# Splitting a weight block before, and not after, the results of the running block are worked on, in a two-layer decoder trunk

## Chip, cores and metric

The kernel runs on one core of a Trainium2 chip (trn2). The metric is the device time of one execution in microseconds. Before the change it is 1976.48 us, the median of three runs (1976.42 to 1977.69).

## What is computed

Two layers of a decoder trunk on 256 tokens of width 1024, all in fp32. Each layer adds a token mixer, a cross attention and a feed-forward part to the residual x:

```python
for layer in range(2):
    h = rms_norm(x, norm_mix[layer])
    x = x + token_mixer(h, ...)              # h @ w_in, four branches A to D, gates, w_branch, w_out
    h = rms_norm(x, norm_cross[layer])
    m = rms_norm(mem, norm_mem[layer])
    x = x + memory_cross_attention(h, m, w_xq[layer], w_xkv[layer], w_xo[layer])
    h = rms_norm(x, norm_ffn[layer])
    x = x + (swiglu(...) if layer == 0 else moe_ffn(...))     # dense, d_ff 3584; then top 2 of 8 experts
return rms_norm(x, norm_final)
```

The branches of the mixer are A sliding-window attention, B attention over 64 selected keys per query, C retention and D pooling. Nearly all the work is the products of 256 token rows with weight matrices, some 530 MB of fp32 that are read once.

## The kernel before

**Blocks.** The weights come in blocks of 512 rows by 512 columns, 128 partitions by 2048 fp32 or 1 MB. `plan_chunks` and `plan_dense` write out their order: 60 mixing blocks of layer 0, 42 dense blocks, 60 mixing blocks of layer 1, and then the experts' jobs. All of the first 162 stand in `PLANNED`; block n uses slot n mod 6 of the buffers `raw` and `w_hi`.

**Precision.** A product is made of three fast matmuls. ScalarE copies a block to the rounded type, w_hi (`hi`, L871, signalled by `hi_done`). VectorE writes the rest, raw less w_hi, back in place (`lo`, L1391, `lo_done`). The moving or stationary operand, kept in `stat0` and `stat1`, is split the same way. TensorE then adds x_hi w_hi, x_hi w_lo and x_lo w_hi (`product`, L2254 to L2256): 24 matmuls for a block (32 for the eight "turned" chunks xk0 to xk3 and xq0 to xq3 of each layer, L2629 and L2631).

**What sets the order.** Each engine runs its own program in its order. TensorE counts finished blocks in `block_used`. SP's queue issues the load of block n+5 as soon as block n-1 is used up (`load_block`, L628 and L629), since that frees the slot. `hi` of block n+5 waits for its landing and for the same count. SP does nothing else in between, apart from a few loads of small inputs.

**A step.** For each block n ScalarE and VectorE have a step. It consists of the work on results that belongs to it and of the split of block n+5 (`LEAD` is 5). The work is written out by hand in `work` (L1068) and `dense_work` (L1208) for ScalarE and in `work_of` (L1758) and `dense_work` (L1924) for VectorE. It holds, for instance:

- evacuating the accumulators of a chunk once its last block is used up (`evac`, `gates_out`, `gated`, `residual`, and `rotate` for the rotary chunks);
- the steps of softmax between TensorE's small matmuls (`soft_start`, `exps`, `soft_end` with the scaling L1631, `soft_out` with the copy L1640);
- splitting operands that TensorE has just transposed (`split_gain` L1463, `split_pair` L1495, `split_mem` L1503, `split_pool` L1472, `hidden_split` L1921), which later blocks or the next one use.

TensorE does its small matmuls and transposes at fixed places: in the middle of a block (`within`, `dense_within`) or behind it (`after`). Before each it waits for the bank (`opened`, `emptied`) or the operand (`ready`). Small results share four banks in turn, so a bank can be used again only when its reader of four uses before is through. Examples that matter below:

- xo1's second block turns x's first half in its middle (f0, f1); the dense block g0 behind it waits for them to be split. f2 and f3 are turned behind g0's first block and waited for by its second.
- d5's second block turns the last hidden units in its middle, and d6 uses them. d6's second block turns h0 and h1, and layer 1's first block, pu, waits for these.
- xk0 uses the memory rows, split in the steps of upA1 and upB1; its second half waits for the latter.
- behind upD0 TensorE makes the scores of a1; its second pair of banks needs the copy of a0's output.
- xkv3's second block is followed by xo0, which uses xt0 and xt1; xo1's first block is followed by xo0's second, which uses xt2 and xt3.

ScalarE's loop over a layer's blocks ends like this (L1338 to L1350), and VectorE's (L2199 to L2212) is built in the same way:

```python
for c, i in ORDER:
    if c.name in TURNED:
        hi_planned(layer * LAYER_BLOCKS + c.numbers[i] + LEAD)
    work(layer, c.name, i)
    ...
    if c.name not in TURNED and (layer, c.name, i) != (DEPTH - 1, "xo1", 1):
        hi_planned(layer * LAYER_BLOCKS + c.numbers[i] + LEAD)
```

So only the turned chunks split block n+5 first. From block 162 on `hi_planned` splits the first experts' blocks; VectorE's splits of those stand in `first_expert_lows` with a lead of four, and `lo_planned` does nothing there.

Of the kernel before, what the change touches and what calls it, by code (L numbers as in the profile page):

```python
# [50 lines left out]
TURNED = [f"x{w}{n}" for w in "kq" for n in range(4)]  # L51
SLOTS = 6
CYCLE = 6
LEAD = 5
# [97 lines left out]
def build(nc, x_in, mem_in, positions, norm_mix, w_in, attn_sink, w_branch, w_out, pool_w, pool_scale,  # L152
          norm_cross, norm_mem, w_xq, w_xkv, w_xo, norm_ffn, dense_w_gu, dense_w_down, router_w,
          moe_w_gu, moe_w_down, norm_final, out):
    DEPTH, D = norm_mix.shape
# [13 lines left out]
    MIX_BLOCKS = len(ORDER)  # L169
    FFN_BLOCKS = UNITS * UNIT_BLOCKS  # L170
    LAYER_BLOCKS = MIX_BLOCKS + FFN_BLOCKS
# [7 lines left out]
    with ctx:  # L179
# [314 lines left out]
        def dense_block(which, u, i):  # L494
            return (0, MIX_BLOCKS + DENSE.index((which, u, i)))
# [81 lines left out]
        def used_at(b):  # L577
            return number(b) + (1 + SLOTS)
# [287 lines left out]
        def _(act):  # L866
            def hi(b, width=UNIT):

                act.wait_ge(raw_landed[slot(b)], landed_at(b))
                act.wait_ge(block_used, number(b) + 1)  # L870
                act.activation(w_hi[:, slot(b), :, 0:width], raw[:, slot(b), :, 0:width], ACT.Copy).then_inc(hi_done, 1)  # L871

            def expert_hi_of(b):

                act.wait_ge(raw_landed[slot(b)], landed_at(b))
                act.wait_ge(block_used, number(b) + 1)
                act.activation(expert_hi(b), expert_raw(b), ACT.Copy).then_inc(hi_done, 1)  # L877

            def hi_planned(n):

                if n >= len(PLANNED):
                    expert_hi_of((EXPERTS_BASE, n - len(PLANNED)))
                    return
                layer, c, i = PLANNED[n]
                if layer == "dense":
                    hi((0, n))
                    return
                if c.name == "kv":
                    act.wait_ge(kv_landed[i], (layer + 1) * 16)
                if c.name[:3] in ("upA", "upB"):  # L890
                    act.wait_ge(up_landed[int(c.name[3])], (2 * layer + "AB".index(c.name[2]) + 1) * 16)
                hi((0, n), c.n)
# [9 lines left out]
            def norm_scale(layer, name, junk):  # L902
                square_sum(x, junk, norm_act, layer, f"{name} sq")
                root_of_mean(norm_act, norm_dve, layer, f"{name} sq")

            def split_gain(layer, name, dst, kind, q):

                act.wait_ge(small_full.sem, full_at(layer, name))
                for i, k in enumerate((2 * q, 2 * q + 1)):
                    ins = act.activation(dst[:, 0, k, :], small(layer, name)[:, i * T:(i + 1) * T], ACT.Copy,  # L910
                                         scale=gain_at(layer, kind, k))
                ins.then_inc(act_hi.sem, 1)
# [295 lines left out]
            def dense_work(which, u, i):  # L1208

                if (which, u, i) == ("u", 0, 0):  # L1210
                    split_gain(0, "f2", stat0, "ffn", 2)
                    split_gain(0, "f3", stat0, "ffn", 3)
                    norm_scale(0, "ffn", tok)
                if which == "g" and i == 1:
                    if u == 0:
                        act.wait_ge(norm_dve.sem, norm_dve.at(0, "ffn inv"))
                    else:
                        act.wait_ge(dense_hid.sem, dense_hid.at(u - 1, "hid"))
                    act.wait_ge(block_used, used_at(dense_block("g", u, 1)))
                    for t in range(NT):  # L1220
                        ins = act.activation(silu_g[:, t, :], bank[t][:, :], ACT.Silu, scale=rs_ffn[:, t:t + 1])
                    ins.then_inc(dense_silu.sem, 1)
                    if u:
                        hidden_turned(u - 1, 4)
                if (which, u, i) == ("d", UNITS - 2, 1):
                    hidden_turned(UNITS - 1, 0)
                if (which, u, i) == ("d", UNITS - 1, 1):
                    split_gain(1, "h0", stat0, "mix", 0)
                    split_gain(1, "h1", stat0, "mix", 1)

            def hidden_turned(u, first):

                act.wait_ge(dense_tr.sem, dense_tr.at(u, "tr"))
                for t in range(NT):
                    src = bank[first + t][:, :].rearrange("p (k n) -> p k n", k=4)
                    ins = act.activation(hidden_t(0, u)[:, :, t * P:(t + 1) * P], src, ACT.Copy)
                ins.then_inc(dense_hi.sem, 1)
# [99 lines left out]
            hi_planned(4)  # L1337
            for layer in range(DEPTH):  # L1338
                for c, i in ORDER:
                    if c.name in TURNED:  # L1340
                        hi_planned(layer * LAYER_BLOCKS + c.numbers[i] + LEAD)
                    work(layer, c.name, i)
                    if layer == 0:
                        first_layer_extras(c.name, i)
                    if c.name not in TURNED and (layer, c.name, i) != (DEPTH - 1, "xo1", 1):
                        hi_planned(layer * LAYER_BLOCKS + c.numbers[i] + LEAD)
                if layer == 0:
                    for n, step in enumerate(DENSE):
                        dense_work(*step)
                        hi_planned(MIX_BLOCKS + n + LEAD)  # L1350

            act.wait_ge(norm_dve.sem, norm_dve.at(1, "ffn inv"))
            act.activation(tok[:, 0, :], x[:, 0, :], ACT.Copy, scale=rs_ffn[:, 0:1])
# [33 lines left out]
        def _(dve):  # L1387
# [6 lines left out]
            def lo_planned(n):  # L1394

                if n >= len(PLANNED):
                    return
                layer, c, i = PLANNED[n]
                lo((0, n), UNIT if layer == "dense" else c.n)
# [524 lines left out]
            def dense_work(which, u, i):  # L1924

                if (which, u, i) == ("u", 0, 0):
                    split_gain(0, "f2", stat0, "ffn", 2)
                    split_gain(0, "f3", stat0, "ffn", 3)
                    dve.wait_ge(acc_free[CH["xo1"].parity].sem, acc_free[CH["xo1"].parity].at(0, "xo1"))
                    scale_of_rows(x, tok, rs_ffn, norm_dve, norm_act, 0, "ffn ")  # L1930
                if which == "g" and i == 1 and u:
                    hidden_split(u - 1, 4)
                if which == "u" and i == 1:
                    dve.wait_ge(dense_silu.sem, dense_silu.at(u, "silu"))
                    dve.wait_ge(block_used, used_at(dense_block("u", u, 1)))
                    if u:
                        dve.wait_ge(dense_tr.sem, dense_tr.at(u - 1, "tr"))
                    for t in range(NT):
                        ins = dve.scalar_tensor_tensor(out=hid[:, t, :], in0=bank[2 + t][:, :], scalar=rs_ffn[:, t:t + 1],
                                                       in1=silu_g[:, t, :], op0=ALU.mult, op1=ALU.mult)  # L1940
                    ins.then_inc(dense_hid.sem, 1)
                if which == "d":
                    if (u, i) == (UNITS - 2, 1):
                        hidden_split(UNITS - 1, 0)
                    if (u, i) == (UNITS - 1, 1):
                        split_gain(1, "h0", stat0, "mix", 0)
                        split_gain(1, "h1", stat0, "mix", 1)
                    dve.wait_ge(block_used, used_at(dense_block("d", u, i)))
                    for t in range(NT):
                        xs = x[:, t, i * 512:(i + 1) * 512]  # L1950
                        ins = dve.tensor_tensor(xs, xs, bank[4 + 2 * i + t][:, :], ALU.add)
                    ins.then_inc(dense_acc.sem, 1)
# [246 lines left out]
            for layer in range(DEPTH):  # L2199
                for c, i in ORDER:  # L2200
                    if c.name in TURNED:
                        turned_sum(layer, c.name)
                        lo_planned(layer * LAYER_BLOCKS + c.numbers[i] + LEAD)
                    work_of(layer, c.name, i)
                    if c.name not in TURNED:
                        lo_planned(layer * LAYER_BLOCKS + c.numbers[i] + LEAD)
                    if (layer, c.name, i) != (DEPTH - 1, "xo1", 1):
                        first_expert_lows(layer * LAYER_BLOCKS + c.numbers[i])
                if layer == 0:
                    for n, step_ in enumerate(DENSE):  # L2210
                        dense_work(*step_)
                        lo_planned(MIX_BLOCKS + n + LEAD)  # L2212

            route()
            first_expert_lows(len(PLANNED) - 1)
# [671 lines left out]
```

## Time and profile before

| | us |
|---|---|
| median of the runs | 1976.48 |
| the profiled execution | 1977.02 |
| its span, first to last instruction | 1974.8 |
| TensorE's matmuls busy | 1959.9 (99%) |
| VectorE busy | 1534.9 (78%) |
| ScalarE busy | 1251.4 (63%) |
| mixing and dense blocks of the trace | 8 to 1005 |
| experts | 1013 to 1964 |

The span is one execution as the hardware profiler saw it. The time of that execution is 2.2 us longer, for what lies around the instructions. Busy time is an average: what a change is worth is read at the place where it acts, from the waits and the order of events there. In the rows below, L871 is a line of the kernel, PE is TensorE, ACT ScalarE, DVE VectorE, and SPq SP's queue; a bracket at the end of a row gives the engine's idle time before it and what ended that.

### The profile page before, as it was taken

The numbers are of one execution on the slowest core, as the hardware profiler recorded it, in microseconds if no ns is written. First come the engines' busy times: TensorE is split into PE (matmuls) and PEld (weight loads), VectorE is DVE, ScalarE is ACT, GpSimd is POOL, SyncE is SP. The second block draws the span as 40 slices with busy tenths as digits, with TensorE's granted clock in tenths as the row PEclk, the third lists the DMA queues.
The fourth block names the chain that finished last, engine by engine and source line by source line (L and its number), as shares of the span: only waits on it lengthen the run. The fifth ranks groups of instructions, "written<-read, shape, count | busy, mean of one in ns | idle before, by whom it ended". The sixth has DMA issues, their size and how long they took to land.

```text
span 1974.8 us, 25344 instructions
## 1 busy us (share of the span) xinstructions
PE 1959.9 (99%) x9380; PEld 1626.1 (82%) x9380; DVE 1534.9 (78%) x1445; ACT 1251.4 (63%) x1235; POOL 105.7 (5%) x164
## 2 busy tenths in 40 slices
PE   8999999999999999999999999999999999999998
PEld 7887888888888887788878888888888888888886
DVE  7877667655555777777669988989888988988996
ACT  6566545454434456655566777877767776776775
POOL 4300000000000210000000100100000000000030
PEclk9999999999999999999999999999999999999999
DMA  8544655455555544566479999999999999999995
GB/s 290 163 150 149 179 191 171 149 182 188 185 191 182 171 150 156 164 204 215 154 267 362 378 400 382 388 372 379 387 374 397 364 389 386 364 392 380 385 393 201
DMA packets 203698, 539.16 MB, mean 273 GB/s; under 512 B 10265, under 2 KB 34401, under 8 KB 203617
## 3 DMA queue, kind: packets, MB, share of 16 engines
q1 hardware_dynamic: 200784, 529.38, 74.3%
q0 software_dynamic: 2304, 8.39, 1.2%
q8 instruction: 53, 0.87, 0.2%
q10 hardware_dynamic: 528, 0.29, 0.0%
q14 instruction: 29, 0.23, 0.0%
HBM read 529.64 MB, written 8.39 MB: 272 GB/s over the span
## 4 chain that ended last, share of the span: by engine, by line
PE 98%; DVE 1%; ACT 0%; DMA 0%; issue 0%; SPq 0%; DVEq 0%; ACTq 0%
PE bank L2701 15%; PE bank L2699 15%; PE bank L2700 15%; PE bank L2254 13%; PE bank L2256 13%; PE bank L2255 13%; PE bank L2631 3%; PE bank L2302 2%; PE bank L2629 1%; PE bank L2778 1%; PE bank L2320 1%; PE bank L2342 1%; PE bank L2713 0%; PE bank L2711 0%; PE bank L2712 0%; PE bank L2793 0%
## 5 line engine op out<-in xcount | busy, mean ns | idle before, releaser
L877 ACT ACTIVATE w_hi<-raw 128x2048 fp32r<-128x2048 f32 x336 | 628.6, 1922 | 122.5 <-DMA raw<-in_moe_w_gu 80.6
L1410 DVE TENSOR_TENSOR expert_lo<-raw,w_hi 128x2048 fp32r<-128x2048 f32 x280 | 630.2, 2294 | 20.6 <-ACT w_hi L877 20.5
L2699 PE MATMUL bank<-w_hi,stat 128*128 128x512 f32 x1312 | 514.2, 392 | 0.0
L2701 PE MATMUL bank<-w_hi,stat 128*128 128x512 f32 x1312 | 511.0, 390 | 0.0
L1391 DVE TENSOR_TENSOR low_in_place<-raw,w_hi 128x2048 fp32r<-128x2048 f32 (+1 forms) x161 | 367.5, 2285 | 134.9 <-ACT w_hi L871 134.4
L2254 PE MATMUL bank<-w_hi,stat 128*128 128x512 f32 (+1 forms) x1168 | 458.3, 392 | 0.0
L2255 PE MATMUL bank<-low_in_place,stat 128*128 128x512 f32 (+1 forms) x1168 | 453.1, 388 | 0.0
L2256 PE MATMUL bank<-w_hi,stat 128*128 128x512 f32 (+1 forms) x1168 | 453.1, 388 | 0.0
L871 ACT ACTIVATE w_hi<-raw 128x2048 fp32r<-128x2048 f32 (+1 forms) x161 | 305.8, 1904 | 220.5 <-DMA raw<-in_dense_w_gu 60.2
L2700 PE MATMUL bank<-expert_lo,stat 128*128 128x512 f32 x1088 | 423.4, 389 | 0.0
L2701 PEld LDWEIGHTS bank<-w_hi,stat 128*128 128x128 f32 x1312 | 246.2, 188 | 51.6
L2699 PEld LDWEIGHTS bank<-w_hi,stat 128*128 128x128 f32 x1312 | 246.3, 188 | 49.8
L2254 PEld LDWEIGHTS bank<-w_hi,stat 128*128 128x128 f32 x1168 | 219.7, 188 | 49.9 <-issue 6.0
L2256 PEld LDWEIGHTS bank<-w_hi,stat 128*128 128x128 f32 x1168 | 219.7, 188 | 45.2
L2255 PEld LDWEIGHTS bank<-low_in_place,stat 128*128 128x128 f32 x1168 | 219.9, 188 | 42.7
L2700 PEld LDWEIGHTS bank<-expert_lo,stat 128*128 128x128 f32 x1088 | 204.3, 188 | 41.7
L1410 DVE TENSOR_TENSOR area_low<-raw,w_hi 128x2048 fp32r<-128x2048 f32 x56 | 130.2, 2326 | 0.2
L1991 DVE TENSOR_TENSOR stat<-bank,stat 128x512 fp32r<-128x512 f32 x56 | 36.5, 687 | 74.4 <-ACT stat L1277 74.3
L2700 PE MATMUL bank<-area_low,stat 128*128 128x512 f32 x224 | 87.2, 389 | 0.0
L1248 ACT ACTIVATE area<-bank 128x512 f32<-128x512 f32 x56 | 30.9, 596 | 87.8 <-PE bank L2701 87.8
L2631 PE MATMUL bank<-stat,w_hi 128*128 128x512 f32 x256 | 68.7, 395 | 0.0
L844 POOL COPY token_now<-slot_token 128x1 int32 x7 | 13.0, 1860 | 816.0 <-PE bank L2793 589.7
(346 smaller groups left out, 1438.7 us busy)
## 6 DMA issues: line engine op xcount, KB each, us to landing
raw<-in_moe_w_gu SPq DMA_DIRECT2D x224, 1024.0 KB, 7.5
raw<-in_moe_w_down SPq DMA_DIRECT2D x112, 1024.0 KB, 8.4
raw<-in_w_in SPq DMA_DIRECT2D x55, 1024.0 KB, 4.9
raw<-in_dense_w_gu SPq DMA_DIRECT2D x28, 1024.0 KB, 5.1
raw<-in_w_xkv SPq DMA_DIRECT2D x16, 1024.0 KB, 5.3
raw<-in_dense_w_down SPq DMA_DIRECT2D x14, 1024.0 KB, 5.1
raw<-in_w_branch SPq DMA_DIRECT2D x8, 1024.0 KB, 5.0
raw<-in_w_branch SPq DMA_DIRECT2D x16, 512.0 KB, 7.0
```

What stands on the lines that cost most here:

```text
L871: act.activation(w_hi[:, slot(b), :, 0:width], raw[:, slot(b), :, 0:width], ACT.Copy).then_inc(hi_done, 1)
L877: act.activation(expert_hi(b), expert_raw(b), ACT.Copy).then_inc(hi_done, 1)
L1391: dve.tensor_tensor(in_place_lo(b)[:, :, 0:width], raw[:, slot(b), :, 0:width], f32_of(w_hi[:, slot(b), :, 0:width]), ALU.subtract).then_i ...
L1410: dve.tensor_tensor(expert_low(b), expert_raw(b), f32_of(expert_hi(b)), ALU.subtract).then_inc(lo_done, 1)
L2254: pe.matmul(dst, x_hi, wh, start=start, stop=False)
L2255: pe.matmul(dst, x_hi, wl, start=False, stop=False)
L2256: return pe.matmul(dst, x_lo, wh, start=False, stop=stop)
L2302: ins = pe.transpose(b[:, i * P:(i + 1) * P], src, ident[:, :])
L2631: ins = pe.matmul(whole, wh[:, k, cols], moving[:, 0:2, k, :], start=(k == 0), stop=(k == KD - 1))
L2699: pe.matmul(dst[:, :], x_hi, wh[:, at], start=start, stop=False)
L2700: pe.matmul(dst[:, :], x_hi, wl[:, at], start=False, stop=False)
L2701: ins = pe.matmul(dst[:, :], x_lo, wh[:, at], start=False, stop=stop)
```

## The change

In both loops the split of block n+5 now stands ahead of step n's work for all mixing and dense blocks. For the turned chunks nothing changes. Instructions, buffers and semaphores stay what they were, and so do TensorE's, SP's and GpSimd's programs.

```diff
--- before.py
+++ after.py
@@ -1337,17 +1337,15 @@
             hi_planned(4)
             for layer in range(DEPTH):
                 for c, i in ORDER:
-                    if c.name in TURNED:
+                    if (layer, c.name, i) != (DEPTH - 1, "xo1", 1):
                         hi_planned(layer * LAYER_BLOCKS + c.numbers[i] + LEAD)
                     work(layer, c.name, i)
                     if layer == 0:
                         first_layer_extras(c.name, i)
-                    if c.name not in TURNED and (layer, c.name, i) != (DEPTH - 1, "xo1", 1):
-                        hi_planned(layer * LAYER_BLOCKS + c.numbers[i] + LEAD)
                 if layer == 0:
                     for n, step in enumerate(DENSE):
+                        hi_planned(MIX_BLOCKS + n + LEAD)
                         dense_work(*step)
-                        hi_planned(MIX_BLOCKS + n + LEAD)
 
             act.wait_ge(norm_dve.sem, norm_dve.at(1, "ffn inv"))
             act.activation(tok[:, 0, :], x[:, 0, :], ACT.Copy, scale=rs_ffn[:, 0:1])
@@ -2200,16 +2198,14 @@
                 for c, i in ORDER:
                     if c.name in TURNED:
                         turned_sum(layer, c.name)
-                        lo_planned(layer * LAYER_BLOCKS + c.numbers[i] + LEAD)
+                    lo_planned(layer * LAYER_BLOCKS + c.numbers[i] + LEAD)
                     work_of(layer, c.name, i)
-                    if c.name not in TURNED:
-                        lo_planned(layer * LAYER_BLOCKS + c.numbers[i] + LEAD)
                     if (layer, c.name, i) != (DEPTH - 1, "xo1", 1):
                         first_expert_lows(layer * LAYER_BLOCKS + c.numbers[i])
                 if layer == 0:
                     for n, step_ in enumerate(DENSE):
+                        lo_planned(MIX_BLOCKS + n + LEAD)
                         dense_work(*step_)
-                        lo_planned(MIX_BLOCKS + n + LEAD)
 
             route()
             first_expert_lows(len(PLANNED) - 1)
```

## Rows read from the trace of the kernel before

**Rows 1.** The page: busy time by engine; the chain that ended last, by engine

```profile
PE 1959.9 (99%) x9380; PEld 1626.1 (82%) x9380; DVE 1534.9 (78%) x1445; ACT 1251.4 (63%) x1235; POOL 105.7 (5%) x164
...
PE 98%; DVE 1%; ACT 0%; DMA 0%; issue 0%; SPq 0%; DVEq 0%; ACTq 0%
```

**Rows 2.** Waits of TensorE: for what, us in total, times, longest

```profile
PE bank L2302 <- DMA x<-in_x: 3.2, 2, 1.7
...
PE bank L2629 <- DVE stat L1503: 0.5, 2, 0.3
```

**Rows 3.** Timeline, two dense blocks, SP's queue, ScalarE, VectorE (start us, us, what)

```profile
441.18 0.37 SPq L629 DMA_DIRECT2D raw<-in_dense_w_down  x1
...
446.62 0.37 SPq L629 DMA_DIRECT2D raw<-in_dense_w_down  x1
...
446.22 1.92 ACT L871 ACTIVATE w_hi<-raw 128x2048 fp32r<-128x2048 f32 x1 [3.49 <-DMA raw<-in_dense_w_down]
...
448.17 2.29 DVE L1391 TENSOR_TENSOR low_in_place<-raw,w_hi 128x2048 fp32r<-128x2048 f32 x1 [0.26 <-ACT w_hi L871]
```

**Rows 4.** The page's DMA issues: count, size, median us to landing

```profile
raw<-in_dense_w_gu SPq DMA_DIRECT2D x28, 1024.0 KB, 5.1
```

**Rows 5.** Timeline, first dense blocks of layer 0, SP's queue and VectorE

```profile
395.85 0.37 SPq L629 DMA_DIRECT2D raw<-in_dense_w_gu  x1
...
402.18 0.37 SPq L629 DMA_DIRECT2D raw<-in_dense_w_gu  x1
...
399.76 1.66 DVE L1463 SCALAR_TENSOR_TENSOR stat<-bank,gains,stat 128x256 fp32r<-128x256 f32 x4
```

**Rows 6.** Timeline, last dense blocks, SP's queue, ScalarE, VectorE

```profile
608.92 0.37 SPq L629 DMA_DIRECT2D raw<-in_w_in  x1
...
614.97 1.92 ACT L871 ACTIVATE w_hi<-raw 128x2048 fp32r<-128x2048 f32 x1 [1.36 <-DMA raw<-in_w_in]
...
613.64 1.29 DVE L1921 TENSOR_TENSOR stat<-bank,stat 128x512 fp32r<-128x512 f32 x2 [2.02 <-ACT stat L1236]
```

**Rows 7.** Timeline, the end of layer 0's mixing blocks, SP's queue and VectorE

```profile
256.50 0.37 SPq L629 DMA_DIRECT2D raw<-in_w_out  x1
...
262.02 1.29 DVE L1672 TENSOR_TENSOR gate<-bank,gate 128x512 f32<-128x512 f32 x2
263.23 1.66 DVE L1503 SCALAR_TENSOR_TENSOR stat<-memT,gains,stat 128x256 fp32r<-128x256 f32 x4
```

**Rows 8.** Attention in layer 1: VectorE's timeline, then the chain (start us, us)

```profile
746.05 0.68 DVE L1640 COPY o_buf<-bank 128x512 f32<-128x512 f32 x1
...
761.94 2.29 DVE L1631 TENSOR_TENSOR area<-area,sinv 128x2048 f32<-128x2048 f32 x1
...
745.87 2.15 PE bank L2320 x16
...
764.58 2.62 PE bank L2302 x24
...
818.01 1.79 PE bank L2302 x16
```

**Rows 9.** Timeline, cross attention in layer 0, SP's queue and VectorE

```profile
355.58 0.37 SPq L629 DMA_DIRECT2D raw<-in_dense_w_gu  x1
...
364.82 0.37 SPq L629 DMA_DIRECT2D raw<-in_dense_w_gu  x1
...
374.07 1.28 DVE L1495 TENSOR_TENSOR stat<-bank,stat 128x512 fp32r<-128x512 f32 x2
```

**Rows 10.** TensorE's first products, its last matmuls, and the end's stretch with granted clock

```profile
8.18 0.77 PE L2254 MATMUL bank<-w_hi,stat 128*128 128x512 f32 x1
...
12.17 0.39 PE L2254 MATMUL bank<-w_hi,stat 128*128 128x512 f32 x1
...
1965.41 1.88 PE L2815 MATMUL bank<-heads_t,expert_lo 128*128 128x512 f32 x4
...
1960.00:1972.00 12.00, 7.23 (x28) 4.66 (x26) 6.19 (x11) 5.72 (x12) 0.00 (x0) 0.97 0.08 31
```

## Prediction, made before the changed kernel was run

> **What bounds the kernel now.** The page comes first. TensorE is busy for 99% of the span and carries 98% of the chain that ended last [rows 1], so a block of weights costs what its matmuls cost, and the change can gain only where TensorE waits. The waits of TensorE are next. They come to 7.3 us in six entries, and nearly all of it is the wait for the first inputs at the kernel's start (the 3.2 us of [rows 2] and an entry of 2.5 us like it); the largest that a result block sets is the 0.5 us on the split memory rows, L1503 [rows 2]. So the question is not what the change frees, but which of the hidden steps stay hidden.
>
> Then the order of events in one dense block, on which all else rests [rows 3]. The load of block n+5 is issued when block n-1 is used up, at 441.18; the next one, 5.44 us later, marks the end of block n (24 matmuls). The load takes 5.0 us to land: ScalarE's split starts at 446.22, released by the DMA, and takes 1.92 us. VectorE's split starts at 448.17 and takes 2.29 us. The median over the 28 dense loads is 5.1 us [rows 4]. So the split of block n+5 is **not work that lies ready while block n is multiplied**: its data land some 0.4 us before block n ends. That decides the case.
>
> **The change, step by step.** Counted from that issue, ScalarE is through the split at +7.0 us and VectorE at +9.3 us (5.0 + 1.92 + 2.29 and the hand-overs), or 1.5 and 3.8 us after the end of block n. Before, ScalarE and VectorE did step n's results as soon as they were there, and then the split. Afterwards neither touches step n's results before those times. Removed and added instructions: none. Moved: one activation (1.92 us) and one subtraction (2.29 us) per step, for all but the eight turned chunks of each layer, which had this order already. No DMA moves, since a load waits only for its block to be used; SP's and POOL's queues are passed by nothing. The split itself is early by four blocks in either order: free. Behind the new waits stand the evacuations, softmax steps and operand splits of step n, and TensorE waits for these in program order. I walked through its waits; most have a block or more of room. In the steady dense blocks, for instance, the hidden splits end 5.2 us after g's second block and are asked for two blocks (11 us) later: nothing. These have no such room:
>
> 1. **Operands made in the last block before they are used, 19.1 us.** Rows f0, f1 are turned in the middle of xo1's second block, split, and used by the next block. A block with eight transposes takes 6.3 us [rows 5], VectorE's split of the rows 1.66 us [rows 5]. From the issue, the operand is ready at 9.3 + 1.66 = 10.9 us and wanted at 6.3: 4.6 us. The same holds for f2, f3 one dense block on (4.6), and for h0, h1 ahead of layer 1 (4.6). The last hidden units, used by d6, wait for a load that landed only 6.05 us after its issue [rows 6]: 6.05 + 1.92 + 2.29 + 1.29 = 11.6 against 6.3, so 5.3 us.
> 2. **Split of the memory rows for xk0, 7.6 us.** The load is issued at 256.50 [rows 7]; VectorE's split of it would end at 265.8; then come the gating (1.29) and the split (1.66), together until 268.7. They ended at 264.9. TensorE waited for exactly this before (L1503, [rows 2]), so all of 3.8 us shows, in both layers.
> 3. **Attention chains, 8.6 us.** After upD0, TensorE's second pair of score banks (1.1 us into the 2.15 us that begin at 745.87) needs the copy L1640, which began at 746.05 and would now end at 749.0: 2.1 us. The normalised scores of a1 were ready at 764.2 for transposes at 764.58 [rows 8]; with the split ahead of them they come 1.0 us late, beyond the 2.1. For b1 the transposes at 818.01 had 0.2 us of room, and by the same sum come 1.2 us late. Times two layers.
> 4. **Cross attention, 5.2 us.** The split of xt0, xt1 is asked for 9.2 us after the issue of block 60 (355.58 to 364.82, [rows 9]) and is ready at 9.4 + 1.29: 1.6 us. That of xt2, xt3 comes at 10.6 against 8.2 us: 2.4 us. The residual after them adds 0.2. In layer 1 VectorE's expert splits are not moved, only ScalarE's: 1.0 in place of 4.2.
> 5. **Single ones, 2.1 us.** Layer 0's memory transposes need a bank that split_pool frees (1.5 us); layer 1's out0 residual had 0.1 us left (0.6).
>
> The sum is 42.6 us. Where a stall stands, the loads issued before it have landed by its end, so it is not paid twice; I took each from its own issue.
>
> **TensorE's clock** is the one resource that the change may touch and that the middle of the trace doesn't show. At the start the nine products from 8.18 to 12.17 were paced at 0.43 us, the 1.2 GHz level, against 0.226 later: 2.0 us lost. At the end the last matmuls were over at 1967.3, and the mean granted clock of 0.97 in 1960 to 1972 puts the fall to half at about 1971.3, 4.0 us later [rows 10]. Four of the stalls above (4.6, 4.6, 4.6, 5.3) are longer than that, two (3.8) nearly so. Bounds: no fall, nothing, or six falls at twice the price of the start, 24 us. Lying close to the 4.0 us, I take two falls of four, 3.9 us. By the Trainium skill ("TensorE: Matmul & The Clock Gate", "HAM oscillation — how this bites in real kernels"), an engine that waits idle for its data is sent back to the slow clock at every such wait, and pays the warm-up each time. By that rule all four long ones fall, and the sum is 4 us more than mine; no row here shows a stall in mid-kernel that would tell.
>
> The profiled execution took 1977.02 us (span 1974.8, 2.2 around it): 1977.0 + 42.6 + 3.9 = 2023.5. The median is 0.5 lower, so I say 2023.
>
> **The rivals.** *(a) Room everywhere, no change, about 1976.5.* Loads would have to land well before a block's end, or the waits have slack that I overlooked. For it: TensorE now waits hardly anywhere, and of some hundred steps I find a dozen short. Against it: the room at places 2 and 3 is 0 to 0.2 us by the rows, and 3.8 us of delay can't vanish in that. 4%. *(b) Faster or at least not slower.* The split would fill time in which ScalarE and VectorE wait for the block's end, and leave them free right behind it, where the 1.92 and 2.29 us used to stand ahead of the next step. Price: at most the 1.6 us of TensorE's waits that lie behind its start, so 1975. It decides if the load lands more than 4.2 us before the block's end; it lands 0.4 us before it [rows 3]. 2%. *(c) The clock falls at every long stall and takes long to return.* 42.6 + 24 gives 2043. For it the 4.0 us of [rows 10]; against it that matmuls follow without a break, and that a slow stretch gives VectorE time to catch up. It is what the rule of the Trainium skill named above would come to at its worst. 14%. *(d) Only the straight chains of places 1 and 2 stall* (26.7 us), since attention and cross attention take back in the next step what they lose: 2004. 12%. The forecast has 68%.
>
> **How the numbers follow.** The forecast's own range is 2010 to 2034: a fifth of the 42.6 up and down (each stall is a small difference of two long sums), and 0 to 4 falls of the clock. To leave out no more than 2 in 10 the range takes in the nearer half of (c) and of (d): 2007 to 2040. 0.2% (4 us) is about what a measurement can tell. Slower by more than that: the forecast, (c) and (d), 0.94; within it, (a) and most of (b), 0.05; faster, 0.01.
>
> **What would show it.** In the waits of TensorE: new entries for L1503 (7 to 8 us in all), L1463 (14), L1921 (5), L1495 (4 to 6), L1640 (4) and L1631 (4). ScalarE's split then waits on the DMA, and step n's evacuations begin 1.4 us after the block's end. Steady dense blocks keep their 5.44 us. A clock below full speed in the stretches behind f1, f3, d6 and layer 1's pu tells of the falls. I am wrong if TensorE's waits stay under 10 us, or if dense blocks grow all along, which would mean that the results' delay compounds from step to step.

## The result, and the profile after

The changed kernel takes **2047.13 us**, the median of five runs (2045.67 to 2049.09), against 1976.69 for the kernel before in the same comparison: 1.0354 times as long, with a 95% interval of 1.0343 to 1.0366. That is 70.4 us slower, where 46.5 had been forecast; the range ended at 2040. The profiled execution took 2045.9 us, with a span of 2043.7.

The page first: busy time, the chain that ended last, and the two groups of the split (busy, mean ns; after the bar the engine's idle time before them and what ended it).

```profile
PE 1981.5 (97%) x9380; PEld 1639.6 (80%) x9380; DVE 1535.1 (75%) x1445; ACT 1252.6 (61%) x1235; POOL 105.5 (5%) x164
...
PE 89%; DMA 4%; DVE 3%; ACT 2%; SPq 1%; issue 1%; POOL 0%; DVEq 0%; ACTq 0%
...
L1389 DVE TENSOR_TENSOR low_in_place<-raw,w_hi 128x2048 fp32r<-128x2048 f32 (+1 forms) x161 | 370.6, 2302 | 292.6 <-ACT w_hi L871 292.0
L871 ACT ACTIVATE w_hi<-raw 128x2048 fp32r<-128x2048 f32 (+1 forms) x161 | 306.0, 1900 | 461.0 <-DMA raw<-in_w_in 134.0
```

The same two groups on the page of the kernel before:

```profile
L1391 DVE TENSOR_TENSOR low_in_place<-raw,w_hi 128x2048 fp32r<-128x2048 f32 (+1 forms) x161 | 367.5, 2285 | 134.9 <-ACT w_hi L871 134.4
L871 ACT ACTIVATE w_hi<-raw 128x2048 fp32r<-128x2048 f32 (+1 forms) x161 | 305.8, 1904 | 220.5 <-DMA raw<-in_dense_w_gu 60.2
```

The work is the same: VectorE and ScalarE are busy to within 1.2 us of [rows 1], with as many instructions. Their idle time ahead of the splits has more than doubled. And the chain that was TensorE's for 98% is its own for only 89%; DMA, VectorE and ScalarE have entered it. Two numbers split the loss. TensorE's idle time (span less busy) grew from 14.9 to 62.2 us, **47.3 us of waits**. Its busy time grew by **21.6 us** with the same 9380 matmuls, for which a slower clock and the refilling of a stopped engine are the candidates. Together they are the 68.9 us between the spans.

The waits of TensorE (for what; us in total, times, longest). Lines of VectorE's and TensorE's programs stand two to four lower than before the change.

```profile
PE bank L2250 <- DVE stat L1461: 13.7, 3, 4.7
PE bank L2298 <- DVE area L1629: 9.8, 4, 3.9
PE bank L2625 <- DVE stat L1501: 7.7, 2, 3.9
PE bank L2250 <- DVE stat L1919: 5.3, 1, 5.3
PE bank L2316 <- DVE o_buf L1638: 4.7, 2, 2.3
PE bank L2250 <- DVE stat L1493: 4.4, 3, 2.5
...
PE bank L2298 <- POOL gate L799: 2.3, 1, 2.3
```

In [rows 2] the only line of this kind was the memory rows', with 0.5 us. Every line named in the prediction is here, and five of the six come out within an us of their forecast (14, 7 to 8, 5, 4, 4 to 6). The sixth, L1629, was to be 4 and is 9.8.

One dense wait in full, from the timelines of SP's queue, ScalarE, VectorE and TensorE (start us, us, what; a bracket is the idle time before and what ended it). It is the wait for f0, f1, place 1 of the prediction.

```profile
412.95 1.03 PE L2298 MATMUL bank<-ident,x 128*128 128x128 f32 x8
...
415.56 1.91 ACT L871 ACTIVATE w_hi<-raw 128x2048 fp32r<-128x2048 f32 x1 [7.85 <-DMA raw<-in_dense_w_gu]
417.38 1.55 ACT L910 ACTIVATE stat<-bank,gains 128x256 fp32r<-128x256 f32 x4
...
417.50 2.29 DVE L1389 TENSOR_TENSOR low_in_place<-raw,w_hi 128x2048 fp32r<-128x2048 f32 x1 [5.79 <-ACT w_hi L871]
419.71 1.65 DVE L1461 SCALAR_TENSOR_TENSOR stat<-bank,gains,stat 128x256 fp32r<-128x256 f32 x4
...
421.42 0.80 PE L2250 MATMUL bank<-w_hi,stat 128*128 128x512 f32 x1 [4.70 <-DVE stat L1461]
```

ScalarE stood idle for 7.85 us until the load had landed; VectorE waited 5.79 us for ScalarE; only then was the operand split that the next block needed. The rows had been turned by 414.0 (the first line), and the block before ended at 416.7. So ScalarE stood idle for 1.6 us more, and VectorE, which needs ScalarE's part first, for 3.5, while the urgent work lay behind a wait.

**The clock.** The stretches in which the granted clock (PEclk) stood at half, by windows; the columns are the window, its length, busy us of PE, PEld, DVE, ACT and POOL, PEclk, DMA share, GB/s.

```profile
138.00:141.40 3.40, 3.40 (x11) 2.32 (x8) 3.23 (x6) 2.40 (x2) 0.00 (x0) 0.51 0.05 19
213.20:219.90 6.70, 4.88 (x20) 4.59 (x21) 3.97 (x2) 5.04 (x8) 0.00 (x0) 0.50 0.34 129
281.50:288.20 6.70, 5.66 (x18) 4.78 (x19) 2.26 (x5) 1.40 (x1) 0.00 (x0) 0.50 0.00 0
404.40:407.70 3.30, 3.30 (x10) 2.53 (x9) 0.00 (x0) 1.90 (x1) 0.00 (x0) 0.50 0.18 69
421.40:424.70 3.30, 3.28 (x8) 2.61 (x9) 2.06 (x3) 1.91 (x1) 0.00 (x0) 0.50 0.02 5
438.50:445.20 6.70, 5.46 (x13) 4.30 (x14) 3.30 (x8) 3.38 (x3) 0.00 (x0) 0.50 0.16 61
660.40:667.10 6.70, 6.11 (x14) 4.81 (x15) 3.15 (x4) 0.51 (x1) 0.00 (x0) 0.50 0.00 0
680.90:684.20 3.30, 3.30 (x9) 2.57 (x8) 1.94 (x2) 1.86 (x1) 0.00 (x0) 0.50 0.00 0
947.10:950.40 3.30, 3.30 (x11) 2.61 (x11) 0.00 (x0) 0.00 (x0) 2.98 (x5) 0.50 0.24 98
```

Nine falls, each of 3.4 or 6.8 us, 44 us in all. TensorE was busy for 38.7 us of these windows (the PE column added up), so by an estimate half of that, 19 us of the 21.6, went to the clock. This is one execution; the mean granted clock was 0.988 in it and 0.986 to 0.989 in the other four. From 1010 to 2036, through layer 1's last mixing blocks and all experts, TensorE was at full clock and busy for 1024.3 of the 1026 us.

### The profile page after: what moved, and what is told of

The parts are those of the page before. It is cut to its first block, busy times and chain, and to the rows that moved or that the text cites. A ratio compares the mean times of both kernels' runs of the same rounds, so it can differ in the third digit from the quotient of the medians.

```text
span 2043.7 us, 25344 instructions
## 1 busy us (share of the span) xinstructions
PE 1981.5 (97%) x9380; PEld 1639.6 (80%) x9380; DVE 1535.1 (75%) x1445; ACT 1252.6 (61%) x1235; POOL 105.5 (5%) x164
## 4 chain that ended last, share of the span: by engine, by line
PE 89%; DMA 4%; DVE 3%; ACT 2%; SPq 1%; issue 1%; POOL 0%; DVEq 0%; ACTq 0%
PE bank L2697 15%; PE bank L2695 15%; PE bank L2696 15%; PE bank L2250 11%; PE bank L2252 11%; PE bank L2251 11%; PE bank L2627 3%; PE bank L2298 2%; PE bank L2625 1%; DMA raw<-in_w_in 1%; ACT w_hi L871 1%; PE bank L2774 1%; DVE low_in_place L1389 1%; DMA raw<-in_dense_w_gu 1%; DMA raw<-in_w_branch 1%
## 5 line engine op out<-in xcount | busy, mean ns | idle before, releaser
L871 ACT ACTIVATE w_hi<-raw 128x2048 fp32r<-128x2048 f32 (+1 forms) x161 | 306.0, 1900 | 461.0 <-DMA raw<-in_w_in 134.0
L2250 PE MATMUL bank<-w_hi,stat 128*128 128x512 f32 (+1 forms) x1168 | 464.6, 398 | 23.4 <-DVE stat L1461 13.7
L2252 PE MATMUL bank<-w_hi,stat 128*128 128x512 f32 (+1 forms) x1168 | 457.6, 392 | 0.0
L2250 PEld LDWEIGHTS bank<-w_hi,stat 128*128 128x128 f32 x1168 | 222.9, 191 | 77.0 <-DVE stat L1461 14.9
L2252 PEld LDWEIGHTS bank<-w_hi,stat 128*128 128x128 f32 x1168 | 222.4, 190 | 46.5
```

Of the source, the lines that this page charges most:

```text
L2250: pe.matmul(dst, x_hi, wh, start=start, stop=False)
L2252: return pe.matmul(dst, x_lo, wh, start=False, stop=stop)
```

## The experiments

Three theories stood after the result. **Landing**: the whole loss comes from splits that wait for a load which lands just before the block's end, at the few steps whose results have no room. **Order**: results put second are late as such, and the delay compounds. And for the 21.6 us, **clock** against anything else that lengthens matmuls. All ratios below are to the kernel before, run on the same chip, with a 95% interval.

### The same order, one block less ahead

The split of block n+4, whose load was issued one block earlier, stands ahead of step n's work in both loops. Left out below are the same edit in the dense loops and, at the two ends, the split of block 4 that is no longer made ahead of the loops and one that ScalarE makes behind them.

```diff
+PLAN_LEAD = 4
...
-                        hi_planned(layer * LAYER_BLOCKS + c.numbers[i] + LEAD)
+                        hi_planned(layer * LAYER_BLOCKS + c.numbers[i] + PLAN_LEAD)
...
-                    lo_planned(layer * LAYER_BLOCKS + c.numbers[i] + LEAD)
+                    lo_planned(layer * LAYER_BLOCKS + c.numbers[i] + PLAN_LEAD)
```

> The changed order, but each mixing and dense step splits block n+4 instead of n+5, whose load was issued one block earlier and has landed when the step begins. Theory (the damage is the wait for a load that lands only 0.4 us before its block's end): that wait is gone, ScalarE is through the split 1.9 us and VectorE 4.2 us after the issue, which is inside every 6.3 us interval that mattered; TensorE's waits are those of the kernel before (under 10 us), the clock stays full, 1974 to 1981 us. Rival (the 4.2 us of splitting ahead of the results are the damage by themselves): the waits for L1461, L1501 and L1919 remain at 1 to 3 us each and the time is 1990 to 2010.

It took 1977.22 us, ratio 1.0000 (0.9990 to 1.0009). The split first, results second, in every step, and nothing lost. ScalarE's timeline in the dense blocks and, of the waits of TensorE, the memory rows' of [rows 2]:

```profile
409.53 1.92 ACT L872 ACTIVATE w_hi<-raw 128x2048 fp32r<-128x2048 f32 x1
...
PE bank L2625 <- DVE stat L1502: 0.5, 2, 0.2
```

This split has no bracket: it starts right behind ScalarE's own work and waits for no DMA. Others still wait (0.64 us for the next one, at 412.09): over the kernel ScalarE is idle for 174.5 us ahead of its splits, against 461.0 in the changed kernel and 220.5 before. But nothing that TensorE needs is held up by it. So what costs is not the order but the landing that the results have to wait for. *Order* falls, and with it the idea that the split's 4.2 us of work delay the results by themselves; they do so where they can only begin 5 us after the issue.

### ScalarE's loop alone

VectorE keeps the old order; only ScalarE's loop is changed.

> Only ScalarE splits first; VectorE has its order of before. Theory: VectorE's results are late only where ScalarE's were: rows f1, f3, h1 are ready at 7.0 + 1.6 + 0.9 = 9.5 us after the issue instead of 10.9 (3.2 us late, three times), the last hidden units 4 us, the memory rows 1.2 us in each layer, nothing at the copy L1640 nor at a1 and b1. 17 us of waits, and 2 to 8 us of slow clock: 1996 to 2002. Rival (the clock falls as often as in the changed kernel, whatever the stalls' length): over 2010.

It took 2001.68 us, ratio 1.0129 (1.0112 to 1.0146), 24 us of the 70. The waits of TensorE:

```profile
PE bank L2252 <- DVE stat L1461: 9.1, 3, 3.1
PE bank L2252 <- DVE stat L1919: 4.1, 1, 4.1
```

The splits that TensorE waits for are named after VectorE, though VectorE's order is the old one. Its splitting of operands needs the part that ScalarE makes first (L910 above), and that now stands behind the landing. Each of the four long waits is 1.2 to 1.7 us shorter than with both loops changed, and the attention waits (L1629, L1638) are gone: they belonged to VectorE's loop. In their place stand 0.9 us for ScalarE's part of attention (L950). TensorE is idle for 17.4 us more than before, 17 having been expected, and busy for 7.0 us more: three stretches of half clock, of 3.4 us each, behind the waits of 3.12, 4.10 and 2.97 us, and none behind the one of 3.03. The reverse, VectorE's loop alone, wasn't tried.

### The dense blocks alone, and the mixing blocks alone

```diff
                     for n, step in enumerate(DENSE):
+                        hi_planned(MIX_BLOCKS + n + LEAD)
                         dense_work(*step)
-                        hi_planned(MIX_BLOCKS + n + LEAD)
```

The same swap stands in VectorE's loop. The second kernel is the changed one without this swap.

> The changed order in the 42 dense steps alone. Theory (the loss is local, in the last blocks of a chain): TensorE waits only at f3, d6 and layer 1's h1, 4.6 + 5.3 + 4.3 = 14.2 us, with three falls of the clock of 1.7 to 3.4 us each behind them, 7 us: 1995 to 2003. The steady dense blocks keep 5.44 us. Rival (each of the 42 steps pays something): over 2005 and waits spread over the dense stage.

> The changed order in the mixing steps alone, the dense ones as before. Theory: the two stages do not act on each other, so the loss is what the changed kernel lost less what the dense steps lose: 2047.1 - 1998.5 + 1977.3 = 2026, 2020 to 2031, with all waits at L1493, L1501, L1629, L1638 and one of the three at L1461. Rival (stalls in one stage shield the next, since the loads catch up): over 2032.

Dense alone took 1998.17 us, ratio 1.0108 (1.0091 to 1.0125), 20.9 us more; mixing alone 2027.21 us, ratio 1.0250 (1.0233 to 1.0267), 49.9 us more. The sum is 70.8, against 70.4 for both: to within the intervals of 3.4 us that each loss has, they add and don't breed others. The dense part can be read out completely. Its waits of TensorE, then the page's busy time:

```profile
PE bank L2254 <- DVE stat L1463: 9.3, 2, 4.8
PE bank L2254 <- DVE stat L1921: 5.2, 1, 5.2
```

```profile
PE 1966.0 (99%) x9380; PEld 1631.5 (82%) x9380; DVE 1532.4 (77%) x1445; ACT 1251.5 (63%) x1235; POOL 107.0 (5%) x164
```

14.5 us of waits, and 6.1 us by which TensorE is busy for longer than the 1959.9 of before: 20.6 of the 20.9. The 6.1 are half of the 12.2 us that it is busy in the three stretches of half clock, at 407, 625 and 646 us. Three waits did it, and 0.3 us are left for all the other blocks of the 42, as the prediction had said of the steady ones.

### Waits filled with products

To price the clock by itself, TensorE makes products whose results are thrown away while it would wait; nothing of the computation is left out. The first kernel fills the four longest waits (f1, f3, d6, h1), the second nearly all. Of the first one's edit, the helper and one of its places; left out are the other three and, at the dense down blocks, two waits of TensorE that changed places to make room.

```diff
+            def keep_clock_in(b, n):
+                for k in range(n):
+                    pe.matmul(b[:, :].rearrange("p (k n) -> p k n", k=2), stat1[:, 0, 4, 0:P], stat1[:, 0, 4:6, :],
+                              start=True, stop=True)
...
                     if (layer, name, i) == (1, "pu", 0):
+                        keep_clock_in(bank[0], 18)
```

> The changed kernel with 18 to 20 extra products of 512 columns (0.226 us each, 4.1 to 4.5 us) put ahead of the four long waits f1, f3, d6 and layer 1's h1; they write free banks. Theory (22 us of the loss are the half clock behind stalls, of which these four stalls have 20.5 us at half clock): the four falls are gone and the stalls stay as long, 10 us less than the changed kernel, 2034 to 2040. Rival (TensorE's busy time grew for another reason, such as contention for the operands): 2045 or more, since nothing else is taken away.

> The changed kernel with extra products ahead of every wait longer than 2.2 us: the four of the run before and also xk0's (15 each, twice), b1's scores (15, twice), the second pair of a1's score banks (9, twice), xt3 (9) and the turned idx rows (8). Theory: the waits of 48 us stay as they are and the slow clock's 22 us go: 1977.3 + 48 = 2025, 2022 to 2031, and no slow stretch before the end. Rival (a part of TensorE's added busy time is not the clock): 2033 or more, with full clock.

With four filled: 2039.31 us, ratio 1.0316 (1.0299 to 1.0333), 7.8 us less than the changed kernel. With nearly all filled: 2029.18 us, ratio 1.0263 (1.0246 to 1.0281), 17.9 us less. The page of the second, and its window from 200 to 1010:

```profile
PE 2002.1 (99%) x9549; PEld 1657.6 (82%) x9549; DVE 1534.0 (76%) x1445; ACT 1252.0 (62%) x1235; POOL 108.4 (5%) x164
```

```profile
200.00:1010.00 810.00, 803.10 (x3923) 666.11 (x3922) 507.49 (x555) 388.53 (x465) 22.33 (x24) 1.00 0.53 169
```

No fall at all in the window that holds eight of the nine, and none ahead of it; the 169 added products (38.4 us at 0.227 each) leave 1963.7 us for the 9380 of the kernel itself, against 1981.5 in the changed one and 1959.9 before. So **the clock costs about 18 us of the 70 (14 to 22 by the two intervals), and the waits themselves 52**. A wait stays a wait when it is filled: this is a measurement, and it gives back the clock's part alone. Of the 52, 48.4 are waits and fillings (38.4 and 10.0 us more idle time than before), 1.1 more than the unfilled waits. The other 3.8, by which the 9380 matmuls still take longer than before, I put down to TensorE's refilling at each stop (the product behind the stop at 403.01 takes 0.50 us where the others take 0.39); no run separates that. In the first kernel the four half-clock stretches behind the filled waits are gone, 20.5 us of them; of the unfilled waits three lost the clock that had kept it in the changed kernel, and two kept it that had lost it, so that 27 us of such stretches are left of 44.

### Results first where they are due

The other way round: the changed order everywhere but in the steps that the profile shows short of room. First 11 mixing steps in each layer and 5 dense steps, those whose results TensorE waited for in the changed kernel's trace:

```diff
+RESULTS_FIRST = {("bq", 0), ("bq", 1), ("idx", 1), ("upD0", 0), ("gateD1", 1), ("upC1", 0), ("gateA0", 0), ("upB1", 0), ("xkv3", 1), ("xo1", 0), ("xo1", 1),
+                 ("u", 0, 0), ("d", 5, 0), ("d", 5, 1), ("d", 6, 0), ("d", 6, 1)}
```

> The changed order in all steps but 16 kinds (those of idx1, bq0, bq1, upD0, gateD1's and upC1's and gateA0's, upB1, xkv3's and xo1's last blocks, u0's first, and the last four dense blocks), which work on their results first as before. Theory (the loss sits in about 17 places, and the other steps have room): TensorE's waits return to under 10 us, the clock stays full, 1975 to 1982. Rival (the delay compounds over the many steps that still split first): 1990 or more, with waits at L1631 and L1495 that last.

It took 1986.57 us, ratio 1.0047 (1.0030 to 1.0064): a miss, 4.6 us above the upper end. The largest entry that was left in TensorE's waits is 3.3 us for the residual (L1695). VectorE's and TensorE's timelines at its longest:

```profile
387.60 2.29 DVE L1396 TENSOR_TENSOR low_in_place<-raw,w_hi 128x2048 fp32r<-128x2048 f32 x1 [6.06 <-ACT w_hi L873]
389.81 1.28 DVE L1695 TENSOR_TENSOR x<-x,bank 128x512 f32<-128x512 f32 x2
...
391.14 1.09 PE L2311 MATMUL bank<-ident,x 128*128 128x128 f32 x8 [2.38 <-DVE x L1695]
```

This is xo0's residual behind the split, in a step that was not in the list, since TensorE did not wait there in the changed kernel. There, the block in question had been held up first by the 2.5 us for xt2, xt3 and by the half clock from 404: TensorE reached the transposes 12.4 us after the load's issue (400.58 to 412.95), and the residual was done after 11.1. Here it wants them after 8.1 us (380.63 to 388.76), and the residual is done after 10.5. **One stall had covered the next.** The forecast's 0.6 us for layer 1's out0 residual was covered in the same way: the changed kernel shows nothing, and here it is 0.7. The 2.4 us, a half-clock stretch of 3.4 us behind them and smaller waits of the same kind make the miss. Five more steps were added, xo0's second among them:

> As the kernel that works on its results first in 16 kinds of steps and came to 1986.6, with five kinds more: pu's first block, upD1, gateC1's second, out0's second and xo0's second. Those are the places at which TensorE still waited there (the first-half residual 3.3 us, a1's copies 1.1, b1's scores 1.0, h3 0.9, pu's evacuation 0.6) with one fall of the clock behind them. Theory (every loss has its place, nothing compounds): 1976.5 to 1979. Rival: some of it moves to the next step and stays, over 1981.

It took 1977.60 us, ratio 1.0003 (0.9994 to 1.0013), and the waits of TensorE are those of before to within 0.5 us each, the 0.5 us of the memory rows [rows 2] among them. With results first in 37 of the 162 steps, the changed order in all others costs nothing that a measurement can tell (at most 0.13%, 2.6 us, by the interval). The loss has its places, and nothing compounds.

### b1's step alone

The place that the forecast had missed by most: VectorE's split in the step of gateA0 put back behind the work, in both layers, and all else as changed.

```diff
+                    if (c.name, i) != ("gateA0", 0):
+                        lo_planned(layer * LAYER_BLOCKS + c.numbers[i] + LEAD)
                     work_of(layer, c.name, i)
+                    if (c.name, i) == ("gateA0", 0):
+                        lo_planned(layer * LAYER_BLOCKS + c.numbers[i] + LEAD)
```

The changed kernel at this step in layer 1, from the timelines of SP's queue, ScalarE, VectorE and TensorE:

```profile
866.03 0.61 SPq L654 DMA_DIRECT2D raw<-in_w_branch  x1
866.68 0.62 SPq L655 DMA_DIRECT2D raw<-in_w_branch  x1
...
873.94 1.92 ACT L871 ACTIVATE w_hi<-raw 128x2048 fp32r<-128x2048 f32 x1 [3.01 <-DMA raw<-in_w_branch]
...
878.33 2.29 DVE L1629 TENSOR_TENSOR area<-area,sinv 128x2048 f32<-128x2048 f32 x1
...
880.68 1.97 PE L2298 MATMUL bank<-ident,area 128*128 128x128 f32 x16 [3.80 <-DVE area L1629]
```

The block loaded here comes in two halves by two DMAs, each to 64 of the 128 partitions. The trace gives 5.4 us to landing for the first, so it was there at 871.5; the split waited for the second until 873.9, 7.9 us after the first issue and not 5. Then follow, one behind the other, both splits (VectorE's from 875.89) and the scaling of b1's scores. With 2.9 us more until the landing, the forecast's 1.2 us becomes 4.1. The kernel before had shown it. Its page has the halves, and its timelines of SP's queue and ScalarE the same load, 7.7 us from the issue to the split:

```profile
raw<-in_w_branch SPq DMA_DIRECT2D x16, 512.0 KB, 7.0
...
807.16 0.61 SPq L654 DMA_DIRECT2D raw<-in_w_branch  x1
814.82 1.92 ACT L871 ACTIVATE w_hi<-raw 128x2048 fp32r<-128x2048 f32 x1 [1.80 <-DMA raw<-in_w_branch]
```

> The changed kernel, but in the step of gateA0's first block VectorE does b1's softmax end first and splits second, as before. The block split there is upA1, whose load is issued in two halves. Theory (b1 waited 3.9 us and not 1.2 because VectorE waited for the second half): both waits of 3.9 us go, and the slow stretch behind layer 0's with 3.4 us: 11 us less, 2034 to 2039. Rival (b1 is late from the steps before, where the copy L1638 and a1 were late): at least 2 us of each wait remain and the time is over 2041.

It took 2034.98 us, ratio 1.0292 (1.0275 to 1.0309), 12.2 us less. The waits of TensorE and VectorE's timeline at the same step:

```profile
PE bank L2301 <- DVE area L1629: 2.2, 2, 1.1
```

```profile
862.34 2.29 DVE L1629 TENSOR_TENSOR area<-area,sinv 128x2048 f32<-128x2048 f32 x1
867.90 4.66 DVE L1389 TENSOR_TENSOR low_in_place<-raw,w_hi 128x2048 fp32r<-128x2048 f32 x2 [3.27 <-ACT w_hi L871]
```

The scaling now ends at 864.6, 3.3 us before VectorE gets a block to split. Of L1629's 9.8 us the 7.7 of b1 are gone and a1's 2.2 are left. TensorE is idle for 8.3 us less and busy for 5.0 less. Not all of the 5.0 belongs to this edit. The half clock behind layer 0's b1 is gone, but so is the one behind a0's copy, whose wait stayed (2.20 us, and 2.35 in the changed kernel), and the one behind xk0 in layer 0 lasted 3.4 us in place of 6.8. So the 7.7 us of waits are b1's for certain, and the 12.2 hold some chance.

## Why the prediction was right or wrong

**Direction and cause: right.** The step on which it rested, that the load of block n+5 lands 0.4 us before block n ends, holds (in the changed kernel one is issued at 448.09, ScalarE's split starts behind it at 453.14, and the next issue is at 453.53). The kernel with the split one block less ahead shows it to be the cause. Steady dense blocks lost nothing.

**Place 1** (f1, f3, h1 at 4.6 each, d6 at 5.3): measured 4.7, 4.6, 4.3 and 5.3. **Place 2** (3.8 twice): 3.9 and 3.9. **Place 4** (1.6 and 2.4): 1.4 and 2.5, and in layer 1 0.5 in place of 1.0. **Place 3**, the bank behind upD0 (2.1 twice) and a1 (1.0 twice): 2.3 and 2.3, 1.0 and 1.1. **Place 5**: the 1.5 for layer 0's memory transposes did not show. 2.3 stood earlier, where the index rows are turned, and this step the prediction had left out. The wait is named after GpSimd (L799), but GpSimd's adds took as long before (last section); they begin 3.2 us late, because VectorE's rotation ahead of them stands behind the split, at 40.61 where it was at 37.42. The 0.6 for layer 1's out0 did not show either, covered by earlier stalls. So the total of the waits, 47.3 for 42.6, owes something to luck: 2.3 us left out of the sum stand against 2.1 that did not come.

**The step that failed for the waits** is b1 in place 3: "by the same sum come 1.2 us late". The sum had the landing of a whole block, 5 us, and this block comes in two halves, the second there after 7.9. It is 3.9 and 3.8, which makes 5.3 us over both layers, more than the whole difference between 42.6 and 47.3. [Rows 4] stood for dense loads, and I carried their 5.1 us to a block of another form, although the page before gave 7.0 us for these halves.

**The term that was mis-sized is the clock**: two falls of 2.0 us, 3.9, where nine falls and the refilling cost 21.6, and the filled kernel regained 18 of them. The falls came behind all waits of 3.8 us and more but one (the 3.80 at 880.7), where I had asked for more than the 4.0 us of the kernel's end [rows 10]. They came behind two of four waits between 2.2 and 2.5 us, where I had expected none. And each lasted 3.4 or 6.8 us. The error was to read the end of the kernel, one fall behind one stop, as a threshold. The price of the start, 2.0 us, was read from the pace of its products; the granted clock over the first 12 us reads 1.00, so no row shows the clock there. In mid-kernel the products have the same pace of 0.43 us, with the granted clock at 0.50. My upper bound of 24 us was right in size by luck, as six falls of 4 us and not nine of 1.6 to 3.1 (half of the busy times above), and its chance was too low: rival (c), 2043, was nearest at 14%, and the range cut it in half. The rule of the Trainium skill that was weighed there ("TensorE: Matmul & The Clock Gate", "HAM oscillation — how this bites in real kernels") says it of a kernel whose TensorE waits some 3 to 5 us for a DMA ahead of each tile: each of these waits sends the clock back. The trace agrees for seven of the eight waits from 3.8 to 5.3 us, and not for the one of 3.80; the two falls behind shorter waits are outside what the Trainium skill tells there. The 4 us that I let the rule add were too few because I applied it to the four longest waits alone.

**The rivals.** (a) and (b) fell with the first page. (d), waits only in the straight chains, fell: attention and cross attention hold 19 of the 47 us. What would have shown me wrong, a delay that grows from step to step, did not come.

The sum in the terms of the profiled execution: 1977.0 + 47.3 + 21.6 = 2045.9.

## What to carry to other kernels

Before work that waits for a DMA is moved ahead of other work, look up when that DMA lands against when the work behind it is wanted: what the others pay is the landing and the moved work behind it, here 5 us and 4.2, and not the 4.2 alone. Take the landing from the loads of that very block, the last part of it where it comes in parts. And where TensorE is the bound, price a stop at its length and, where the clock falls, at 1.6 to 3.1 us more; here that was nearly every stop from 3.6 us up and about half of those from 2.1 to 2.6; after mending the stops that the profile shows, look again, for each may have covered one behind it.

## What the runs showed of the hardware

**A fall can begin after the wait is over.** TensorE's timeline of the changed kernel at the wait for the copy L1638:

```profile
137.24 1.33 PE L2316 MATMUL bank<-heads_t 64*128 64x256 f32 x8 [2.35 <-DVE o_buf L1638]
...
139.09 0.63 PE L2251 MATMUL bank<-low_in_place,stat 128*128 128x512 f32 x1
139.52 0.63 PE L2252 MATMUL bank<-w_hi,stat 128*128 128x512 f32 x1
```

The small matmuls run again from 137.24, the clock is at 1.2 GHz from 138.0, the products start 0.43 us apart, and from 141.57 they are back at 0.23. In layer 1 the same wait (2.33 us) left the clock alone in this kernel, and took it along in the one with four waits filled (2.16 us): for waits of this length the same code goes either way. All stretches in mid-kernel in these runs last 3.4 or 6.8 us. Counted over the profiled executions of all runs, the filled waits and those for the kernel's first inputs left out, the clock fell behind 25 of 26 waits of 3.6 to 5.3 us, 3 of 4 of 2.9 to 3.2, 9 of 16 of 2.1 to 2.6, and none of 17 of 1.0 to 1.6.

**Two loads of 64 partitions are slower than one of 128.** Half a megabyte each, issued 0.65 us apart, the second half of the block at b1's step was there 2.4 us behind the first. While the second landed, the DMA moved 203 GB/s; in the last 2.6 us of a whole block's load it moved 310 (windows of the changed kernel). Size alone is not the reason: the page has 5.0 us for the ten loads of 512 KB that go to all 128 partitions. Why it is so, no run shows.

```profile
871.50:873.90 2.40, 2.40 (x12) 2.00 (x11) 0.00 (x0) 0.00 (x0) 0.00 (x0) 1.00 0.92 203
450.50:453.10 2.60, 2.60 (x13) 2.15 (x12) 0.00 (x0) 0.20 (x1) 0.00 (x0) 1.00 0.80 310
```

**GpSimd's add varies more than fourfold.** Two adds of the same shape in the changed kernel (GpSimd's timeline), and VectorE's split at the time of the second:

```profile
41.83 0.88 POOL L809 TENSOR_TENSOR gate<-area 128x320 f32<-128x320 f32 x1 [22.23 <-DVE area L1527]
...
42.94 4.15 POOL L809 TENSOR_TENSOR gate<-area 128x320 f32<-128x320 f32 x1
...
42.96 2.28 DVE L1389 TENSOR_TENSOR low_in_place<-raw,w_hi 128x2048 fp32r<-128x2048 f32 x1
```

The slow one begins with VectorE's subtraction of 128x2048. Behind that VectorE goes on with another instruction that reads two inputs (L1412, 128x1024), and the add ends 0.7 us after that one. In layer 1 the subtraction stands alone; there the add takes 3.03 us, and ends 0.7 us after it. In the kernel with results first in 16 kinds of steps the large add begins 0.4 us ahead of the subtraction: it takes 0.87 us, the subtraction 2.64, and GpSimd's small add behind it (128x64) 2.37 in place of 0.32. The Trainium skill ("GPSIMD Engine Reference", "1. Specifications") lists GpSimd's memory interface as shared with VectorE, in contention with its two-input instructions, and these rows fit that. This did not cause TensorE's 2.3 us of waiting for the index rows: in the kernel before, where TensorE does not wait there, the same add took as long.

```profile
39.75 4.16 POOL L809 TENSOR_TENSOR gate<-area 128x320 f32<-128x320 f32 x1
```
